# Placing the experts' rows tile by tile inside the output stage

## The chip, the cores and the metric

The kernel runs on one core of one Trainium2 chip, in one launch. The metric is the device time of that launch in microseconds (us). The core has five engines that run side by side, each taking its own instructions in order: TensorE (PE, matmuls; PEld is its loading of weights), VectorE (DVE), ScalarE (ACT), GpSimd (POOL) and SyncE (SP), which here only issues DMAs. ACT and POOL issue some DMAs too. The engines meet through semaphores.

## The reference, cut to what matters

Two layers run over 1024 latent tokens and 256 context tokens. In each, attention is merged and projected, and then every token goes through a mixture of experts: the best of 4 groups, the two best of its 8 experts, 32 experts in all. The last layer needs the 1024 latent tokens only.

```
x = x + mod[:, 2] * merge_branches(ya, yb, yc, gates, P)
h2 = modulate(rms_norm(x), mod[:, 3], mod[:, 4])
g_idx = argmax(h @ w_rg); e_in_group = (h @ w_re)[its group]
top_v, top_i = lax.top_k(e_in_group, 2)
w = softmax(top_v) * g_w
order = argsort(flat_e); xs = h[order // 2]
y = (silu(xs @ w_gate[e]) * (xs @ w_up[e])) @ w_down[e]
x = x + mod[:, 5] * segment_sum(y * w, tok)
```

## The kernel before

Tokens are worked on in tiles of 128 rows: nq = 10 tiles in layer 0, nq = 8 in layer 1. Each layer has a stage of projections, one of attention, one that merges the branches, and the experts' stage, `stage_experts`. That last one has four blocks, and all engines meet at the end of a block:

1. `output_and_route` (L1630). For each tile t PE does 48 matmuls of the output projection (L1806; L1793 for the first tile). DVE multiplies by the gate (L1752) and adds the residual (L1755), ACT squares (L1727) and takes the root (L1730), DVE scales and shifts (L1766, L1769): that is h, the experts' input. POOL stores it (L1707). PE transposes h (L1816), ACT copies the transpose (L1718), PE multiplies it by the router (L1824), and DVE copies the 36 logits away (L1743). PE's order is: output(t), router products of tile t-2, transposes of tile t-1. The first pair of tiles is written out, the next ones run in a hardware loop of two tiles a turn; layer 0's last two tiles (context) are written out again.
2. `deal_rows` (L1851). When the logits of all tiles are there, DVE chooses the experts of all tokens in wide instructions of up to 320 elements, PE counts with small matmuls how many rows stand before each (L1996), and DVE works out each row's place. A job is 128 rows of one expert. Job e < 32 holds the first 128 rows of expert e; the jobs behind hold what goes beyond 128. POOL then writes each token's number to its place in the DRAM table `token_of`, with one indirect DMA per tile and choice (L2010), 20 in layer 0 and 16 in layer 1. The first expert's weights are loaded meanwhile.
3. `run_experts` (L2024). Job by job: POOL loads 128 token numbers (L2105) and gathers their rows of h (L2110), PE transposes them (L2224) and multiplies (L2232 for gate and up, L2246 for down). The weights are split into a high part (ACT, L2137) and a low part (DVE, L2185; a quarter of all, the second half of down, by POOL, L2122), so that three passes give the precision wanted. SP loads the next weights (L2085) as soon as the split has freed their buffer. The jobs come in pairs, the number of pairs is read from memory by each engine at the start (`load_count`). There are 74 jobs in both layers together.
4. `combine` (L2277): gathers both results of each token and adds them up.

Far ahead of this, POOL clears the result table `ye` in the attention stage of layer 0 (L761): 52 DMAs of 512 KB. The same DMA engines carry the loads of that stage, which SP issues: keys (L774), queries (L777), values (L782). The scores' matmuls are L852.

## Time and profile before

| | us |
|---|---|
| median of 3 runs (5578.72 to 5581.25) | 5580.46 |
| the profiled execution | 5575.79 |
| its span | 5574.2 |
| PE busy, share of span | 4813.2 (86%) |
| DVE busy | 3091.8 (55%) |
| ACT busy | 2596.6 (47%) |
| POOL busy | 1159.4 (21%) |

The profiled execution is one run, whose span is what the trace covers. A row of the timeline gives the start, the length, the engine, the line of the kernel, what is written from what, and in brackets how long the engine stood idle before it and which event ended that.

### The profile page before, as it was taken

Reading aid. Unit: us, or ns where it says so; the run is one execution under the profiler, and the core shown is the slowest. Engines: PE = TensorE matmul, PEld = TensorE weight load, DVE = VectorE, ACT = ScalarE, POOL = GpSimd, SP = SyncE. Lnnn points to the kernel's source line nnn. Section 1 sums busy time; section 2 is a strip of 40 time slices with the busy share of each in tenths; the row PEclk is TensorE's granted clock in tenths of the full one; section 3 lists DMA queues with packets and bytes.
Section 4 is the critical chain, followed back from the end, with each engine's and each line's share of the span. In section 5 each row is a group of like instructions: output and inputs, shape, how many; then the busy total and the mean of one; then the engine's idle time right before and its main releaser. Section 6 shows DMA issues by size and latency. Waiting matters only on the chain. (4 is left out here: it accounts for less than half of the span.)

```text
span 5574.2 us, 82058 instructions
## 1 busy us (share of the span) xinstructions
PE 4813.2 (86%) x28941; PEld 4151.0 (74%) x28941; DVE 3091.8 (55%) x4784; ACT 2596.6 (47%) x3436; POOL 1159.4 (21%) x1097
## 2 busy tenths in 40 slices
PE   5788889889799986899992888999989998599994
PEld 0688878779687875787772888998878777487773
DVE  1655145666544443777766551557663433677775
ACT  0444245556423321777762442555652322477773
POOL 0444200340000001333333441004200000333332
PEclk7899999999899997999996999999989998799997
DMA  8533462313433364899986533424153325799997
GB/s 371 193 94 97 165 213 59 80 47 100 155 124 145 143 217 144 332 397 397 397 330 239 171 95 92 109 57 109 50 159 132 134 90 205 259 397 397 397 397 285
DMA packets 597494, 1111.13 MB, mean 199 GB/s; under 512 B 112560, under 2 KB 295632, under 8 KB 589104
## 3 DMA queue, kind: packets, MB, share of 16 engines
q1 hardware_dynamic: 551760, 956.16, 49.4%
q0 software_dynamic: 29504, 94.50, 4.3%
q10 hardware_dynamic: 16032, 57.88, 2.6%
q8 instruction: 119, 1.95, 0.1%
q14 instruction: 79, 0.65, 0.0%
HBM read 907.97 MB, written 200.45 MB: 199 GB/s over the span
## 5 line engine op out<-in xcount | busy, mean ns | idle before, releaser
L658 PE MATMUL project_proj_acc<-project_w_split,project_hT 128*128 128x256 f32 x5472 | 726.8, 293 | 0.0
L658 PEld LDWEIGHTS project_proj_acc<-project_w_split,project_hT 128*128 128x128 f32 x5472 | 696.2, 199 | 0.3 <-issue 0.2
L1538 PE MATMUL merge_acc<-merge_hT,merge_w_split 128*128 128x512 f32 (+1 forms) x2880 | 641.3, 377 | 36.4 <-DMA merge_hT<-hT 30.4
L1538 PEld LDWEIGHTS merge_acc<-merge_hT,merge_w_split 128*128 128x128 f32 x2880 | 506.6, 191 | 146.7 <-issue 29.7
L2185 DVE TENSOR_TENSOR experts_w_gate<-experts_raw_gate,experts_w_gate 128x2048 fp32r<-128x2048 f32 x148 | 373.5, 2531 | 356.1 <-ACT experts_w_gate L2137 355.9
L937 DVE TENSOR_REDUCE attend_stat<-attend_scores 128x1 f32<-128x1280 f32 (+2 forms) x288 | 305.9, 1062 | 325.2 <-PE attend_scores L852 324.2
L2122 POOL TENSOR_TENSOR experts_w_down<-experts_raw_down,experts_w_down 128x2048 fp32r<-128x2048 f32 x74 | 361.4, 4884 | 534.3 <-ACT experts_w_down L2137 534.3
L837 PE MATMUL attend_out_acc<-attend_values,attend_probsT 128*128 128x64 f32 x3904 | 468.3, 271 | 0.1
L837 PEld LDWEIGHTS attend_out_acc<-attend_values,attend_probsT 128*128 128x128 f32 x3904 | 459.3, 192 | 0.4 <-ACT attend_probsT L882 0.4
L2232 PE MATMUL experts_gate_acc<-experts_w_gate,experts_rowsT 128*128 128x512 f32 x1776 | 438.2, 402 | 12.3 <-DVE experts_rowsT L2190 6.0
L2246 PE MATMUL experts_result_acc<-experts_w_down,experts_hiddenT 128*128 128x512 f32 x1776 | 436.8, 401 | 12.2 <-DVE experts_w_down L2185 12.2
L2232 PE MATMUL experts_up_acc<-experts_w_up,experts_rowsT 128*128 128x512 f32 x1776 | 426.3, 395 | 0.0
L882 ACT COPY attend_probsT<-attend_scores 128x1024 f32<-128x1024 f32 (+1 forms) x288 | 216.5, 752 | 409.3 <-PE attend_scores L826 409.3
L2232 PEld LDWEIGHTS experts_gate_acc<-experts_w_gate,experts_rowsT 128*128 128x128 f32 x1776 | 331.1, 190 | 101.7 <-issue 19.1
L2137 ACT CAST experts_w_gate<-experts_raw_gate 128x2048 fp32r<-128x2048 f32 x148 | 282.3, 1912 | 264.2 <-DMA experts_raw_gate<-in_w_exp_gate_dram 193.0
L2246 PEld LDWEIGHTS experts_result_acc<-experts_w_down,experts_hiddenT 128*128 128x128 f32 x1776 | 330.6, 189 | 88.5 <-issue 12.6
L2232 PEld LDWEIGHTS experts_up_acc<-experts_w_up,experts_rowsT 128*128 128x128 f32 x1776 | 333.2, 188 | 81.2
L852 PE MATMUL attend_scores<-attend_keys,attend_queries 128*128 128x256 f32 (+2 forms) x1344 | 327.1, 358 | 63.9 <-DMA attend_queries<-qk 49.8
L1707 POOL DMA_DIRECT2D h<-experts_h_tile x18 | 9.8, 542 | 1663.0 <-DVE experts_h_tile L1769 1663.0
L2185 DVE TENSOR_TENSOR experts_w_up<-experts_raw_up,experts_w_up 128x2048 fp32r<-128x2048 f32 x148 | 331.8, 2283 | 1.2 <-ACT experts_w_up L2137 1.2
L1547 PE MATMUL merge_acc<-merge_yT,merge_w_split 128*128 128x512 f32 (+1 forms) x1440 | 319.3, 371 | 0.0
L1230 POOL TENSOR_TENSOR attend_p<-attend_p,attend_b_stat 128x640 f32<-128x640 f32 (+1 forms) x72 | 121.9, 1693 | 936.7 <-DVE attend_b_stat L1183 936.7
...
## 6 DMA issues: line engine op xcount, KB each, us to landing
experts_raw_gate<-in_w_exp_gate_dram SPq DMA_DIRECT2D x148, 1024.0 KB, 13.9
...
attend_keys<-qk SPq DMA_DIRECT2D x128, 320.0 KB, 5.7
...
```

Of the source, the lines that this page charges most:

```text
L658: m = pe.matmul(acc[s % 4][:, 0:HALF], hT[:, a, k, t * P:(t + 1) * P], w_split[hf][:, c, k, :], start=(i == 0 and k == 0), stop=(i == 2 an ...
L837: m = pe.matmul(acc[b][:, 0:HD], probsT[b][:, j, :], values[hb][:, kt, :], start=(j == 0), stop=(j == sx.n - 1))
L852: m = pe.matmul(scores[b][:, col:col + n * P], queries[hb][:, sx.t * P:(sx.t + 1) * P], keys[hb][:, half, a * P:(a + n) * P], start=(half ...
L882: act.copy(probsT[b][:, 0:n, :], scores[b][:, 0:n * P].rearrange("p (j n) -> p j n", n=P)).then_inc(ca.sem, 1)
L937: dve.tensor_reduce(stat[:, k, 0:1], scores[b][:, sx.cols], AX.X, ALU.max).then_inc(mx.sem, 1)
L1538: m = pe.matmul(acc[:, b, 0:w], w_split[b][:, a, k, :], hT[:, x, k, 0:w], start=(i == 0 and k == 0), stop=(i == 2 and k == KD - 1))
L1547: m = pe.matmul(acc[:, 3 + b, 0:w], w_split[b][:, a, KD + k, :], yT[:, x, b * KB + k, 0:w], start=(i == 0 and k == 0), stop=(i == 2 and k ...
L2122: pool.tensor_tensor(w[DOWN][:, 1, 1, :], raw[DOWN][:, 1, :], w[DOWN][:, 0, 1, :].bitcast(F32), ALU.subtract).then_inc(w_lo_pool.sem, 1)
L2137: act.copy(w[n][:, 0, half, :], raw[n][:, half, :]).then_inc(w_hi[n].sem, 1)
L2185: dve.tensor_tensor(w[n][:, 1, half, :], raw[n][:, half, :], w[n][:, 0, half, :].bitcast(F32), ALU.subtract).then_inc(w_lo[n].sem, 1)
L2232: m = pe.matmul(acc[:, :], xT[:, a, half * (KD // 2) + k, :], w[n][:, c, half, k * EH:(k + 1) * EH], start=(half == 0 and i == 0 and k == ...
L2246: m = pe.matmul(acc_y[:, c0 * 512:(c0 + 1) * 512], hT[:, a, half * (HK // 2) + k, :], w[DOWN][:, c, half, k * D + c0 * 512:k * D + (c0 + 1 ...
```

## The change

The clearing loop runs over the jobs 32 to 51 in place of 0 to 51: 20 DMAs instead of 52.

What was the block `deal_rows` is spread over its neighbours. In the output stage DVE now chooses the experts of tile t-1 (`choose`, 20 steps and a copy) and places tile t-2 (`place`, 7 steps), each step waiting for the one before it; PE does two small matmuls per tile that count (`ranks`); POOL writes the first 128 rows of each expert to the table, two indirect DMAs per tile (`scatter`). A row beyond 128 is sent to a spare part of the table instead. PE's transposes of tile t-1 now stand in the middle of output(t), and its router products right behind it. SP loads the router's constants ahead of the loop, and the first gate and up weights at its end; the first down weights follow in the next block.

In `run_experts` DVE counts the jobs first (`count_jobs`), then splits, and works out the places of the rows beyond 128 (`deal_beyond`) after the first splits; POOL writes them (`scatter_beyond`), two indirect DMAs after each of the pairs 1 to nq. The weights of the results are worked out at the end (`weights`).

```diff
         if clear_results:
             pool.memset(zeros[:, :], 0.0).then_inc(zeroed.sem, 1)
             pool.wait_ge(zeroed.sem, zeroed.done(0))
-            with pool.Fori(0, MAX_JOBS) as j:
+            with pool.Fori(NE, MAX_JOBS) as j:
                 pool.dma_start(scr["ye"][ds(j * P, P), :], zeros[:, :]).then_inc(cleared.sem, 16)
-            pool.wait_ge(cleared.sem, cleared.done(MAX_JOBS - 1))
+            pool.wait_ge(cleared.sem, cleared.done(MAX_JOBS - NE - 1))
...
-                deal_rows(nc, io, scr, l, nq, st, inner, logits, row_of, weight, jobs, more_pairs, raw, raw_in)
+                output_and_route(nc, io, scr, l, nq, st, inner, ident, r, scat, raw, raw_in)
...
+            sp.dma_start(r.small[:, :], io["k_small"]).then_inc(route_in.sem, 16)
+            sp.dma_start(r.token[:, :], io["k_token"]).then_inc(route_in.sem, 16)
+            sp.dma_start(r.aside[:, :, :], io["k_aside"]).then_inc(route_in.sem, 16)
+            sp.dma_start(earlier[:, :], io["k_earlier"]).then_inc(route_in.sem, 16)
             with sp.Fori(1, NL // 2) as p:
                 body(p, 0)
             if nq > NL:
                 body(NL // 2, 1)
+            for n in range(2):
+                for half in range(2):
+                    sp.dma_start(raw[n][:, half, :], expert_half(io, l, slice(0, 1), n, half)
+                                 ).then_inc(raw_in[n][half].sem, 16)
...
+            def scatter(t):
+
+                pool.wait_ge(rb.sem, rb.done(t * NB + NB - 1))
+                for c in range(2):
+                    pool.indirect_dma_start(
+                        out=scr["token_of"], out_offset=bass.IndirectOffsetOnAxis(
+                            ap=row_first[:, t, c:c + 1].bitcast(U32), axis=0),
+                        in_=r.token[:, t:t + 1], in_offset=None).then_inc(scat.sem, 16)
...
+                    if later(t, 2):
+                        scatter(t - 2)
...
+            pool.wait_ge(route_in.sem, route_in.done(3))
+            for p in range(nq // 2):
+                body(p, 0)
+            scatter(nq - 2)
+            scatter(nq - 1)
...
+            def choose(t, b):
+                n = [0]
+                def step(ins):
+                    ins.then_inc(ra.sem, 1)
+                    dve.wait_ge(ra.sem, ra.done(t * NA + n[0]))
+                    n[0] += 1
+                lgt, s, hot = logit[b], scratch[b], r.hot
+                g = lgt[:, 0:NG]
                 dve.wait_ge(lm.sem, lm.done(t))
-                dve.tensor_copy(logits[:, ds(t, 1), :].rearrange("p o n -> p (o n)"), lg[b][:, 0:N_ROUTE]
-                                ).then_inc(lc.sem, 1)
+                dve.tensor_copy(lgt[:, :], lg[b][:, 0:N_ROUTE]).then_inc(lc.sem, 1)
+                dve.wait_ge(lc.sem, lc.done(t))
+                step(dve.tensor_reduce(best[b][:, 0:1], g, AX.X, ALU.max))
+                step(dve.scalar_tensor_tensor(out=group[b][:, :], in0=g, scalar=best[b][:, 0:1],
+                                              in1=r.small[:, C_PICK4:C_PICK4 + NG], op0=ALU.is_equal, op1=ALU.mult))
+                step(dve.tensor_reduce(pick[b][:, 0:1], group[b][:, :], AX.X, ALU.max))
+                step(dve.tensor_scalar(group[b][:, :], group[b][:, :], pick[b][:, 0:1], 1.0, ALU.is_equal, ALU.subtract))
...
+                for c in range(2):
+                    chosen = hot[:, ds(t, 1), c, :].rearrange("p o n -> p (o n)")
+                    step(dve.tensor_reduce(best[b][:, 1 + c:2 + c], masked[b][:, :], AX.X, ALU.max))
+                    step(dve.scalar_tensor_tensor(out=s[:, :], in0=masked[b][:, :], scalar=best[b][:, 1 + c:2 + c],
+                                                  in1=r.small[:, C_PICK32:C_PICK32 + NE], op0=ALU.is_equal, op1=ALU.mult))
+                    step(dve.tensor_reduce(pick[b][:, 1 + c:2 + c], s[:, :], AX.X, ALU.max))
+                    step(dve.tensor_scalar(chosen, s[:, :], pick[b][:, 1 + c:2 + c], None, ALU.is_equal))
+                    if c == 0:
+                        step(dve.scalar_tensor_tensor(out=masked[b][:, :], in0=chosen, scalar=-3e30,
+                                                      in1=masked[b][:, :], op0=ALU.mult, op1=ALU.add))
+                hots = [hot[:, ds(t, 1), c, :].rearrange("p o n -> p (o n)") for c in range(2)]
+                if later(t, 2):
+                    dve.wait_ge(rk.sem, rk.done(t - 2))
+                step(dve.tensor_tensor(both[b][:, :], hots[0], hots[1], ALU.add))
+                if later(t, 1):
+                    dve.wait_ge(rk.sem, rk.done(t - 1))
+                step(dve.tensor_tensor(seen[b][:, :], seen[1 - b][:, :], both[b][:, :], ALU.add))
...
+                assert n[0] == NA, n[0]
+            def place(t, b):
+                n = [0]
+                def step(ins):
+                    ins.then_inc(rb.sem, 1)
+                    dve.wait_ge(rb.sem, rb.done(t * NB + n[0]))
+                    n[0] += 1
+                rank = r.rank[:, ds(t, 1), :].rearrange("p o c -> p (o c)")
+                row = r.row[:, ds(t, 1), :].rearrange("p o c -> p (o c)")
+                dve.wait_ge(rk.sem, rk.done(t))
+                step(dve.tensor_tensor(two[b][:, :, :], lg[b][:, RANK].unsqueeze(1).to_broadcast([P, 2, NE]),
+                                       r.hot[:, ds(t, 1), :, :].rearrange("p o c n -> p (o c) n"), ALU.mult))
+                step(dve.tensor_reduce(rank, two[b][:, :, :], AX.X, ALU.add))
+                step(dve.tensor_tensor(row, rank, first[b][:, :, 0], ALU.add))
...
+                step(dve.tensor_copy(row_first[:, ds(t, 1), :].rearrange("p o c -> p (o c)"), first[b][:, :, 3]))
+                assert n[0] == NB, n[0]
...
-                        take(t - 2, b)
+                        place(t - 2, b)
+                    if later(t, 1):
+                        choose(t - 1, 1 - b)
...
+            choose(nq - 1, 1)
+            place(nq - 2, 0)
+            place(nq - 1, 1)
+            dve.tensor_copy(r.total[:, :], lg[1][:, TOTAL]).then_inc(tot.sem, 1)
...
+                    if hf == 0:
+                        transposes(t - 1, 1 - b)
...
+            def ranks(t, b):
+                pe.wait_ge(ra.sem, ra.done(t * NA + NA - 5))
+                pe.matmul(lg[b][:, RANK], r.earlier[:, :], both[b][:, :], start=True, stop=False)
+                m = pe.matmul(lg[b][:, RANK], r.ones[:, :], seen[1 - b][:, :], start=False, stop=True)
+                if isinstance(t, int) and t == nq - 1:
+                    m = pe.matmul(lg[b][:, TOTAL], r.ones[:, :], seen[b][:, :], start=True, stop=True)
+                m.then_inc(rk.sem, 1)
...
                     if isinstance(t, int) and t == 0:
                         first_output()
+                        pe.wait_ge(const_in.sem, const_in.done(1))
                     else:
                         output(p, b)
-                    if isinstance(t, int) and t == 1:
-                        pe.wait_ge(const_in.sem, const_in.done(1))
+                        products(t - 1, 1 - b)
                     if later(t, 2):
-                        products(t - 2, b)
-                    if later(t, 1):
-                        transposes(t - 1, 1 - b)
+                        ranks(t - 2, b)
             body(0, 0)
             body(1, 0)
             with pe.Fori(2, NL // 2) as p:
...
+            for half in range(2):
+                sp.dma_start(raw[DOWN][:, half, :], expert_half(io, l, slice(0, 1), DOWN, half)
+                             ).then_inc(raw_in[DOWN][half].sem, 16)
...
+            def scatter_beyond(t):
+                for c in range(2):
+                    pool.indirect_dma_start(
+                        out=scr["token_of"], out_offset=bass.IndirectOffsetOnAxis(
+                            ap=row_beyond[:, t, c:c + 1].bitcast(U32), axis=0),
+                        in_=r.token[:, t:t + 1], in_offset=None).then_inc(scat2.sem, 16)
...
+            pool.wait_ge(scat.sem, scat.done(2 * nq - 1))
             gather(0, 0, 0)
             gather(1, 1, 0)
-            pairs(pool, n_pairs, body)
+            n_pairs = load_count(pool)
+            body(0, False)
+            pool.wait_ge(dealt.sem, dealt.done(0))
+            for i in range(1, nq + 1):
+                body(i, False)
+                scatter_beyond(i - 1)
+            body(nq + 1, False)
+            pool.wait_ge(scat2.sem, scat2.done(2 * nq - 1))
+            with pool.Fori(nq + 2, n_pairs - 1) as i:
+                body(i, False)
+            body(n_pairs - 1, True)
...
+            def count_jobs():
+                step(dve.memset(one_row[:, :], 1.0))
+                step(dve.tensor_tensor(more[:, :, :], r.total[:, :].unsqueeze(2).to_broadcast([P, NE, NT - 1]),
+                                       r.small[:, C_TILE + 1:C_TILE + NT].unsqueeze(1).to_broadcast([P, NE, NT - 1]),
+                                       ALU.is_gt))
...
+                dve.tensor_copy(more_pairs[:, :], pairs_f[:, 0:1]).then_inc(counted.sem, 1)
+            def deal_beyond():
+                step(dve.tensor_tensor(beyond[:, :], tiles_sum[:, :], tiles[:, :], ALU.subtract))
+                step(dve.tensor_tensor(beyond[:, :], beyond[:, :], r.small[:, C_JOB:C_JOB + NE], ALU.subtract))
+                step(dve.tensor_scalar(beyond[:, :], beyond[:, :], float(NE - 1), float(P), ALU.add, ALU.mult))
+                step(dve.tensor_tensor(r.hot[:, :, :, :].rearrange("p t c n -> p (t c) n"),
+                                       r.hot[:, :, :, :].rearrange("p t c n -> p (t c) n"),
+                                       beyond[:, :].unsqueeze(1).to_broadcast([P, 2 * nq, NE]), ALU.mult))
...
+                dve.tensor_copy(row_beyond[:, :, :].rearrange("p t c -> p (t c)"), f[3]).then_inc(dealt.sem, 1)
...
+            count_jobs()
             split(GATE, 0)
+            rows_lo(0)
             split(UP, 0)
-            rows_lo(0)
+            deal_beyond()
+            n_pairs = load_count(dve)
             pairs(dve, n_pairs, body)
+            weights()
```

PE, layer 0, tiles 1 and 2 of the output stage, before. out_acc is the output projection, hT_acc the transposes, logit_acc the router's products:

```order
L1806 MATMUL experts_out_acc<-experts_w_out,experts_mT 128x512 x48
L1816 MATMUL experts_hT_acc<-experts_ident,experts_h_tile 128x128 x8
L1806 MATMUL experts_out_acc<-experts_w_out,experts_mT 128x512 x48
L1824 MATMUL experts_logit_acc<-experts_w_router,experts_hT_tile 128x36 x8
L1816 MATMUL experts_hT_acc<-experts_ident,experts_h_tile 128x128 x8
```

The same tiles after the change:

```order
L1938 MATMUL experts_out_acc<-experts_w_out,experts_mT 128x512 x24
L1950 MATMUL experts_hT_acc<-experts_ident,experts_h_tile 128x128 x8
L1938 MATMUL experts_out_acc<-experts_w_out,experts_mT 128x512 x24
L1958 MATMUL experts_logit_acc<-experts_w_router,experts_hT_tile 128x36 x8
L1938 MATMUL experts_out_acc<-experts_w_out,experts_mT 128x512 x24
L1950 MATMUL experts_hT_acc<-experts_ident,experts_h_tile 128x128 x8
```

The transposes of tile 0 moved from behind the 48 matmuls of tile 1 to between their halves, and likewise for each tile after.

DVE in the loop of the output stage, after the change, from the end of one tile's h to the start of `choose`. The names behind "waits" are those under which a semaphore was first used, and mean nothing here; what matters is which rows wait:

```order
L1891 TENSOR_TENSOR experts_h_tile<-experts_h_tile,experts_shift_rows 128x1024 [waits project0_hT_hi]
L1855 ISA [waits project0_heads_stored1]
L1855 TENSOR_TENSOR experts_two<-experts_logit_acc,experts_hot 128x64
L1849 ISA
L1857 ISA [waits modulation_c_loaded]
L1857 TENSOR_REDUCE experts_rank<-experts_two 128x2
L1849 REGISTER_ALU
L1858 REGISTER_ALU [waits modulation_c_loaded]
L1858 TENSOR_TENSOR experts_row<-experts_rank,experts_first 128x2
L1849 REGISTER_ALU
L1859 SCALAR_TENSOR_TENSOR experts_first<-experts_rank,experts_row 128x2 [waits modulation_c_loaded]
```

Before, one copy (L1743) stood here. Now 27 steps and the copy do, with a register instruction between each two, since the number that a step waits for depends on the loop's turn; at some steps the register instruction itself waits, as at L1858.

POOL in the experts' jobs, after the change, pair 1 and the start of pair 2:

```order
L2117 TENSOR_TENSOR experts_w_down<-experts_raw_down,experts_w_down 128x2048
L2100 DMA experts_index<-token_of 128x1
L2105 DMA experts_rows<-h,experts_index 128x1024
L2117 TENSOR_TENSOR experts_w_down<-experts_raw_down,experts_w_down 128x2048
L2092 DMA token_of<-experts_token,experts_row_beyond 9216x1 x2
L2100 DMA experts_index<-token_of 128x1
L2105 DMA experts_rows<-h,experts_index 128x1024
```

The two scatters (L2092) stand between a subtraction and the next load of token numbers; before, nothing stood there.

## Rows read from the trace of the kernel before

**Rows 1.** Windows: busy us per engine, granted clock, DMA share, GB/s

```profile
2072.00:2166.00 94.00, 94.00 (x484) 78.90 (x482) 35.50 (x48) 15.87 (x28) 3.73 (x7) 1.00 0.54 177
...
2204.00:2232.00 28.00, 0.00 (x0) 0.00 (x0) 0.71 (x4) 0.00 (x0) 18.24 (x19) 0.50 0.02 0
...
2283.00:2320.00 37.00, 36.83 (x174) 29.83 (x173) 34.10 (x18) 28.52 (x21) 17.39 (x7) 1.00 1.04 395
```

**Rows 2.** Timeline, layer 0, from the last h to the first job

```profile
2172.77 1.22 DVE L1769 TENSOR_TENSOR experts_h_tile<-experts_h_tile,experts_shift_rows 128x1024 f32<-128x1024 f32 x1
...
2180.79 0.20 DVE L1743 COPY experts_logits<-experts_logit_acc 128x36 f32<-128x36 f32 x1 [6.58 <-PE experts_logit_acc L1824]
...
2202.91 1.03 POOL L2010 DMA_INDIRECT token_of<-experts_token,experts_row_of  x1 [20.61 <-DVE experts_ended L1973]
...
2227.02 0.96 POOL L2010 DMA_INDIRECT token_of<-experts_token,experts_row_of  x1 [0.31 <-issue]
...
2247.88 8.38 PE L2232 MATMUL experts_gate_acc<-experts_w_gate,experts_rowsT 128*128 128x512 f32 x24 [2.36 <-DVE experts_rowsT L2190]
...
2256.11 5.76 PE L2232 MATMUL experts_up_acc<-experts_w_up,experts_rowsT 128*128 128x512 f32 x24
```

**Rows 3.** Timeline, layer 1, the same places

```profile
4729.52 1.23 DVE L1769 TENSOR_TENSOR experts_h_tile<-experts_h_tile,experts_shift_rows 128x1024 f32<-128x1024 f32 x1
...
4777.48 0.96 POOL L2010 DMA_INDIRECT token_of<-experts_token,experts_row_of  x1 [0.30 <-issue]
...
4798.43 8.02 PE L2232 MATMUL experts_gate_acc<-experts_w_gate,experts_rowsT 128*128 128x512 f32 x24 [2.36 <-DVE experts_rowsT L2190]
```

**Rows 4.** Timeline, layer 0, output stage in its loop

```profile
2074.80 0.16 DVE L1760 RECIPROCAL experts_norm_stat<-experts_norm_stat 128x1 f32<-128x1 f32 x1 [0.27 <-ACT experts_norm_stat L1730]
2075.17 1.28 DVE L1766 SCALAR_TENSOR_TENSOR experts_h_tile<-experts_x_tile,experts_norm_stat,experts_scale_rows 128x1024 f32<-128x1024 f32 x1 [0.20 <-DVE experts_norm_stat L1760]
...
2083.39 1.23 DVE L1752 TENSOR_TENSOR experts_x_tile<-experts_out_acc,experts_gate_in_rows 128x1024 f32<-128x1024 f32 x1 [5.58 <-PE experts_out_acc L1806]
...
2086.07 1.01 ACT L1718 COPY experts_hT_tile<-experts_hT_acc 128x1024 f32<-128x1024 f32 x1 [11.30 <-PE experts_hT_acc L1816]
...
2088.17 0.15 DVE L1757 TENSOR_SCALAR experts_norm_stat<-experts_norm_stat 128x1 f32<-128x1 f32 x1 [2.29 <-ACT experts_square L1727]
...
2091.25 0.19 DVE L1743 COPY experts_logits<-experts_logit_acc 128x36 f32 x1
...
2097.26 1.23 DVE L1752 TENSOR_TENSOR experts_x_tile<-experts_out_acc,experts_gate_in_rows 128x1024 f32<-128x1024 f32 x1 [5.82 <-PE experts_out_acc L1806]
```

**Rows 5.** Timeline, a small DVE step of the block that deals the rows

```profile
2185.49 0.20 DVE L1914 TENSOR_TENSOR experts_g_exp<-experts_g_exp,experts_small 128x40 f32<-128x40 f32 x1
```

**Rows 6.** One line of DVE: ns min/median/max, first and last start

```profile
L1183 DVE TENSOR_SCALAR attend_b_stat<-attend_b_stat,attend_lambda x72: 256/273/278, 1014.7 to 3974.4; 128x1 f32<-128x1 f32 x72
```

**Rows 7.** Timeline, layer 0, tile 1 of the output stage

```profile
2044.33 11.75 PE L1806 MATMUL experts_out_acc<-experts_w_out,experts_mT 128*128 128x512 f32 x48
...
2055.95 1.23 DVE L1769 TENSOR_TENSOR experts_h_tile<-experts_h_tile,experts_shift_rows 128x1024 f32<-128x1024 f32 x1
...
2057.32 1.06 PE L1816 MATMUL experts_hT_acc<-experts_ident,experts_h_tile 128*128 128x128 f32 x8 [1.24 <-DVE experts_h_tile L1769]
```

**Rows 8.** One line, the clearing DMAs; columns as in rows 6

```profile
L761 POOL DMA_DIRECT2D ye<-attend_zeros x52: 531/531/740, 649.9 to 692.1; - x52
```

**Rows 9.** Timeline, attention of layer 0: SP's loads and PE behind them

```profile
733.56 20.38 SPq L774 DMA_DIRECT2D attend_keys<-qk  x4
...
761.63 2.49 PE L852 MATMUL attend_scores<-attend_keys,attend_queries 128*128 128x512 f32 x6 [16.35 <-DMA attend_queries<-qk]
...
765.09 1.49 PE L852 MATMUL attend_scores<-attend_keys,attend_queries 128*128 128x512 f32 x6
```

**Rows 10.** Timeline, experts' jobs of layer 0, POOL and DVE

```profile
2283.43 4.48 DVE L2185 TENSOR_TENSOR experts_w_up<-experts_raw_up,experts_w_up 128x2048 fp32r<-128x2048 f32 x2
...
2283.76 2.82 POOL L2110 DMA_INDIRECT experts_rows<-h,experts_index  x1 [5.79 <-DMA experts_index<-token_of]
...
2325.80 4.94 POOL L2122 TENSOR_TENSOR experts_w_down<-experts_raw_down,experts_w_down 128x2048 fp32r<-128x2048 f32 x1 [6.15 <-ACT experts_w_down L2137]
```

285 lines of the change are left out of this document (118 added, 167 removed).

## The prediction

> **What bounds the kernel now.** I read four views, in this order.
>
> The windows show three kinds of stretch [rows 1]. In the output stage PE is busy without a gap (94.00 of 94 us) and DVE is busy 35.50 us of them: PE bounds it. In the 28 us before the first job PE does nothing and POOL alone works. In the jobs themselves the DMA share is full, 395 GB/s, and PE nearly so: they run at the rate of the DMA, and a faster engine gains nothing there.
>
> The timeline of the handover gives the piece that the change attacks [rows 2, 3]. In layer 0 the last h ends at 2172.77 + 1.22 = 2173.99, and the first gate product starts at 2247.88: 73.9 us in which each step waits for the one before. Of them 6.8 go by until the last logits, 22.1 until the first scatter, 24.1 for the other 19 scatters (last start 2227.02, 1.27 us apart), and 20.9 from the last start to the first product. In layer 1 the same way is 4730.75 to 4798.43, 67.7 us.
>
> The timeline of one tile [rows 4] gives DVE's room: tile to tile 97.26 - 83.39 = 13.87 us, of which DVE stands 5.82 waiting for PE, so its own chain takes 8.05 us. The waits for ScalarE within that chain are not room: DVE takes its instructions in order.
>
> The waits of PE, largest first, lead to the attention of layer 0 [rows 8, 9]: 16.35 us for queries whose key loads SP took 20.38 us to hand over. 52 clears of 0.524 MB were issued from 649.9 to 692.1; that is 27.3 MB, 69 us at 395 GB/s [rows 1], and SP's loads queue among them.
>
> **The change, part by part.** All times are the profiled execution's, 5575.8 us; the median of the runs is 4.7 us (0.08%) above it, and I add the difference at the end.
>
> *Clearing.* 32 clears fewer are 16.8 MB, 42 us of DMA time ahead of the moment when PE wants the queries. The wait of 16.35 goes whole. With it goes part of a slow restart: the first 6 matmuls behind it take 2.49 us, the next 6 take 1.49. Together -17.3. Bounds: 0 (the wait has another cause) and -20 (some more slow matmuls).
>
> *Start of the output stage, a cost.* PE started tile 1 at 2044.33 and ran it through, 11.75 us; the h of tile 0 was ready at 2055.95 + 1.23 = 2057.18, so the transposes, behind all 48 matmuls, waited 1.24 [rows 7]. Now they stand after 24. PE is there at 2050.2 and waits until 2057.8 (0.6 later, for two memsets and a cast that DVE does first). After 7.6 us of idling I take PE at the lower clock (1.2 GHz; the granted clock is 0.50 in the idle stretch of rows 1): the 8 transposes, 1.06 at full clock, take 2.0, and the next 24 matmuls 8.4 as in the first gate product, against 5.76 for the 24 behind it [rows 2]. Tile 1 ends at 2068.2 instead of 2056.1. Router products of tile 0 (1.7) and tile 2 (12.3) follow: 2082.2, where it was 2069.5 (2083.39 less one period of 13.87). **+12.7 us**, in each layer, since the stage is the same code. Bounds: 8 (clock stays high, part absorbed later) and 13.
>
> *DVE in the loop, a cost.* A step of 40 elements takes 0.20, one with 1 element 0.15 [rows 4, 5], and starts 0.04 after the one before. A scalar from memory adds 0.06 (0.273 with two of them against 0.15 [rows 6]). `choose` is the copy and 20 steps: 7 tiny, 12 of 32, 2 of 64 elements, 7 of them with such a scalar: 4.3, and 21 gaps of 0.04: 5.1. `place` is 2 steps of 64 and 5 tiny: 1.5. Less the old copy, 0.2: +6.4. In the loop nine of a tile's register instructions wait themselves. The one of the trace that does (between L1760 and L1766) leaves 0.20 idle instead of 0.04 [rows 4]; other such places leave less, and I take 0.13: +1.1. In return ScalarE's copy of the transposes (1.01, just ahead of the square [rows 4]) moves to a time when it is idle: -0.65. DVE's chain becomes 8.05 + 6.4 + 1.1 - 0.65 + 0.1 for the branch = 15.0 us against PE's 13.87. DVE bounds the loop: +1.15 a tile. That is 6 tiles in layer 0, **+7**, and 5 up to the last tile in layer 1, **+6**. Written-out tiles (8, 9 of layer 0) have no register instructions: 13.9, level with PE. Bounds per tile: 0 (PE still sets the pace) and +3.5 (all 27 register instructions show at 0.13).
>
> *Behind the last h.* Place(7) and choose(8) take 6.6, then the last logits are there (7.0 after h, as before), choose(9) ends at 12.1, place(8) and place(9) at 15.1. POOL starts its last four scatters at 13.7, 15.0, 16.3, 17.5 after h. From the last start to the first product it took 20.9; the loading of the count now stands behind the gathers: 19.9. So the first product comes 37.4 after the last h instead of 73.9. In layer 1, with choose(6) and place(5) at the loop's price, 38.1 instead of 67.7. That is **-36.5** and **-29.6**. Counting the jobs and the first split on DVE, 4 + 4.5 us, lie in the 19.9; splitting up and `deal_beyond`, 4.5 + 4, lie behind the first gate product, 8.4, and what follows it.
>
> *In sum to the first product.* The last h moves by 12.7 + 7 - 0.65 = +19 in layer 0 and 12.7 + 6 - 0.65 = +18 in layer 1. Layer 0: -36.5 + 19 = -17.5. Layer 1: -29.6 + 18 = -11.6.
>
> *In the jobs.* `scatter_beyond` adds two scatters to 10 and 8 pairs, 2.5 us of POOL each at 1.27. POOL stood idle 6.15 before a subtraction that is PE's next need [rows 10]. The DMA moves no more than a few KB. I take +1.5 over both layers for gathers that come late; bounds 0 and 20. Setup of stages: nothing, the weights of the results are worked out while PE does the last down products.
>
> Sum: -17.3 - 17.5 - 11.6 + 1.5 = -44.9. 5575.8 - 44.9 = 5530.9, and by the median 5580.5 - 44.9 = 5535.6. I say **5536**.
>
> **Where a rule and the rows part.** The gap of 0.20 where a register instruction waits, against 0.04 [rows 4], is what makes DVE the bound. The Trainium skill, "VectorE: DVE Perf Modes", section "The DRAIN you can't avoid", says that a semaphore after each operation costs nothing extra. By that the chain would be 13.9, PE would keep the pace, and the sum would be rival 1's.
>
> A gather that POOL issued while DVE was in a 4.48 us pair of two-input subtractions took 2.82 us instead of about 1 [rows 10]. The Trainium skill, "SBUF — State Buffer", section "SBUF: two separate sides", says that GpSimd and such a DVE operation take turns at one port pair, for the whole instruction. By it each scatter in the jobs may be held until a subtraction ends: rival 4's way.
>
> **Rivals.**
>
> 1. *PE keeps the pace in the loop.* For it: 27 small steps and a register instruction that runs beside the step before would be hidden. Against: the 0.20. It gives 13 less: 5523.
> 2. *DVE is dearer than thought:* every register instruction shows. 18 more of 0.13 in 11 tiles are 26 us: 5562. Against: most stand ahead of a waiting step without waiting themselves.
> 3. *The wait for the queries stays*, since SP is late for another reason. Then 17 are lost: 5553. For it: SP's queue holds many loads of its own there. Against: 27.3 MB of zeros in front of them.
> 4. *Slower than before: the scatters in the jobs.* If each is held 0.96 + 4.48 = 5.4 us, a pair costs 10.9, less the slack of 6.15, times 18 pairs: +85, 5620. It decides from the point where a pair of scatters takes over 6.15 + 45/18 = 8.6 us. Against: one gather shows 2.82, which gives 5.6 a pair, within the slack.
> 5. *The stall at tile 1 is small,* as the clock doesn't fall: 5531.
>
> **How the numbers follow.** Forecast (with 5 in it) 0.55, rival 1 0.15, rival 2 0.12, rival 3 0.12, rival 4 0.06. The forecast's own range is 5526 to 5547. To leave out no more than 2 in 10 the range goes from 5517, a little below rival 1, to 5562, rival 2. A change of 0.2%, 11 us, is about the least that a measurement of this kernel can tell. Only rival 4, or 2 and 3 together, end above 5569: faster 0.92, same 0.04, slower 0.04.
>
> **What would show it.** The attention of layer 0: no wait of PE for queries after the first. Tile 1 of each output stage: PE idle 7 to 8 us before the transposes, then 24 matmuls at half the clock. The loop: 15.0 us from one L1874 to the next, without idle time for PE's products before it. Last h to first gate product: 37 to 38 us. The jobs: about 395 GB/s, as before. It is wrong if the loop's tiles take over 17 us, if the wait for queries is still there, or if PE waits for POOL's low part in the first 24 jobs.

## The result, and the profile after

| | before | after |
|---|---|---|
| median (us) | 5579.6 (4 runs, 5578.7 to 5581.3) | 5680.4 (4 runs, 5678.6 to 5696.4) |
| span of the profiled execution | 5574.2 | 5679.0 |

The change made the kernel 1.9% slower: ratio 1.0187, 95% interval 1.0168 to 1.0205. The forecast was 5536, range 5517 to 5562. Where the 104.8 us between the two spans lie, read from the starts of the h tiles and of the first gate product of each job in both timelines:

| stretch | after minus before (us) |
|---|---|
| up to the first h of layer 0 | -14.6 |
| first to last h, layer 0 | +19.5 |
| last h to first product, layer 0 | -32.5 |
| the 36 jobs of layer 0 (643.2 to 728.5) | **+85.3** |
| last job of layer 0 to first h of layer 1 | +5.0 |
| first to last h, layer 1 | +16.9 |
| last h to first product, layer 1 | -24.3 |
| the 38 jobs of layer 1 (679.8 to 728.2) | **+48.5** |
| what follows | +1.0 |

Outside the jobs 29.0 us were gained. Inside them 133.8 were lost, in the step that the prediction had put at 1.5.

The windows of the kernel after, in the output stage's loop, the handover and the jobs (columns as in [rows 1]):

```profile
2087.00:2163.00 76.00, 70.19 (x370) 57.96 (x369) 54.00 (x171) 11.84 (x20) 12.54 (x15) 1.00 0.63 205
2184.00:2212.00 28.00, 2.00 (x13) 1.78 (x13) 16.34 (x56) 7.64 (x6) 6.83 (x7) 0.50 0.35 116
2400.00:2500.00 100.00, 82.92 (x369) 67.20 (x368) 70.36 (x37) 61.58 (x45) 36.97 (x19) 0.91 1.01 313
```

In the loop PE, busy without a gap before, now is idle 8% of the time. In the jobs the DMA share is still full (1.01), but what it moves fell to 313 GB/s, from 396 in the same 100 us of the kernel before. In this trace a full share says that packets are under way, and not how many bytes come.

The handover of layer 0, and the ends of it in layer 1, in the timeline after (to [rows 2, 3]):

```profile
2177.70 1.22 DVE L1891 TENSOR_TENSOR experts_h_tile<-experts_h_tile,experts_shift_rows 128x1024 f32<-128x1024 f32 x1
...
2196.32 0.96 POOL L1738 DMA_INDIRECT token_of<-experts_token,experts_row_first  x1 [0.30 <-issue]
2200.59 0.58 POOL L2100 DMA_DIRECT2D experts_index<-token_of  x1 [3.32 <-POOLq L1691]
2207.69 1.83 POOL L2105 DMA_INDIRECT experts_rows<-h,experts_index  x1 [6.51 <-DMA experts_index<-token_of]
...
2220.29 8.27 PE L2291 MATMUL experts_gate_acc<-experts_w_gate,experts_rowsT 128*128 128x512 f32 x24 [2.36 <-DVE experts_rowsT L2247]
...
4809.13 1.23 DVE L1891 TENSOR_TENSOR experts_h_tile<-experts_h_tile,experts_shift_rows 128x1024 f32<-128x1024 f32 x1
...
4853.73 2.50 PE L2291 MATMUL experts_gate_acc<-experts_w_gate,experts_rowsT 128*128 128x512 f32 x5 [2.36 <-DVE experts_rowsT L2247]
```

From the end of the last h to the last scatter's start it is 17.4 us, from there to the first product 24.0; 41.4 together, and 43.4 in layer 1.

The jobs are where the time went. The time of a job is taken here from the start of its first gate product to that of the next job's. Before, a job took 18.1 us in the first ten and 18.5 from there on, but for the first two of a layer. After, the jobs whose rows are gathered behind a pair of scatters take 22 to 30 us (ten in layer 0: 28.2, 29.8, 27.9, 29.0, 28.7, 27.6, 26.4, 26.2, 28.1, 24.2; eight in layer 1: 30.1, falling to between 22.3 and 22.9 in the last three), all others 18.1. One such job in the timeline after (to [rows 10]):

```profile
2303.15 2.85 POOL L2092 DMA_INDIRECT token_of<-experts_token,experts_row_beyond  x1 [0.17 <-issue]
...
2306.31 1.87 POOL L2092 DMA_INDIRECT token_of<-experts_token,experts_row_beyond  x1 [0.30 <-issue]
2308.19 0.58 POOL L2100 DMA_DIRECT2D experts_index<-token_of  x1
...
2320.47 0.98 POOL L2105 DMA_INDIRECT experts_rows<-h,experts_index  x1 [11.71 <-DMA experts_index<-token_of]
...
2328.81 1.54 PE L2283 MATMUL experts_rowsT_acc<-experts_ident,experts_rows 128*128 128x128 f32 x6 [7.10 <-DMA experts_rows<-h,experts_index]
```

The two scatters hold POOL for about 5 us. Then the index load, 512 bytes, keeps POOL waiting 11.71 us instead of the 5.79 of [rows 10], the gather goes out late, and PE waits 7.10 for its rows. The DMA view of the same stretch of 200 us, after (GB/s in 40 slices of 5 us, then issues with their median time to landing):

```profile
GB/s 414 416 139 205 349 408 415 411 411 302 310 154 148 188 381 415 415 397 353 265 336 77 249 262 410 414 402 406 326 353 108 225 213 377 417 412 369 378 296 224
...
token_of<-experts_token,experts_row_beyond POOLq DMA_INDIRECT x10, 12.5
experts_index<-token_of POOLq DMA_DIRECT2D x9, 0.5 KB, 11.4
```

Behind each pair of scatters the whole stream of weights breaks down: it stays below 360 GB/s for 15 to 30 us, and its lowest slices of 5 us behind the first four pairs are at 139, 148, 77 and 108 GB/s. In the packet records of this stretch 173 of 17,792 packets of 2 KB took over 1 us (the longest 6.1; the median is 0.084), and 33 of 6,656 packets of 4 KB.

### The profile page after: what moved, and what is told of

Its sections match the earlier page's. It is cut to its first block and busy times, and to the rows that moved or that the text cites. A ratio compares the mean times of both kernels' runs of the same rounds, so it can differ in the third digit from the quotient of the medians.

```text
span 5679.0 us, 82433 instructions
## 1 busy us (share of the span) xinstructions
PE 4842.9 (85%) x28870; PEld 4177.9 (74%) x28870; DVE 3324.0 (59%) x5228; ACT 2593.5 (46%) x3436; POOL 1232.5 (22%) x1101
## 5 line engine op out<-in xcount | busy, mean ns | idle before, releaser
L2242 DVE TENSOR_TENSOR experts_w_gate<-experts_raw_gate,experts_w_gate 128x2048 fp32r<-128x2048 f32 x148 | 513.7, 3503 | 189.9 <-ACT experts_w_gate L2141 189.9
L2305 PE MATMUL experts_result_acc<-experts_w_down,experts_hiddenT 128*128 128x512 f32 x1776 | 459.2, 417 | 12.2 <-DVE experts_w_down L2242 12.2
L2305 PEld LDWEIGHTS experts_result_acc<-experts_w_down,experts_hiddenT 128*128 128x128 f32 x1776 | 349.7, 201 | 92.6 <-issue 12.6
L852 PE MATMUL attend_scores<-attend_keys,attend_queries 128*128 128x256 f32 (+2 forms) x1344 | 324.3, 356 | 48.5 <-DMA attend_queries<-qk 34.4
L894 ACT ACTIVATE attend_probs<-attend_scores,attend_stat 128x1280 f32<-128x1280 f32 (+2 forms) x288 | 284.3, 987 | 53.0 <-DVE attend_stat L945 37.1
```

Source lines behind the costliest of these rows:

```text
L852: m = pe.matmul(scores[b][:, col:col + n * P], queries[hb][:, sx.t * P:(sx.t + 1) * P], keys[hb][:, half, a * P:(a + n) * P], start=(half ...
L894: act.activation(probs[b][:, 0:sx.n * P], scores[b][:, sx.cols], ACT.Exp, scale=SCORE_SCALE, bias=stat[:, s % 4, 1:2], accum_out=stat[:, s ...
L2242: dve.tensor_tensor(w[n][:, 1, half, :], raw[n][:, half, :], w[n][:, 0, half, :].bitcast(F32), ALU.subtract).then_inc(w_lo[n].sem, 1)
L2305: m = pe.matmul(acc_y[:, c0 * 512:(c0 + 1) * 512], hT[:, a, half * (HK // 2) + k, :], w[DOWN][:, c, half, k * D + c0 * 512:k * D + (c0 + 1 ...
```

## The experiments

The theory after this reading, **Q**: the index load stands behind the scatters' slow packets on one queue. Rivals: **P**, POOL's own time for the scatters (the prediction's rival 4); **C**, the scatters' packets slow the other DMAs. From e5 on, **A**, which narrows C: what is slow is 4-byte writes to neighbouring addresses; **W** is its rival, by which 128 writes of 4 bytes cost this wherever they go. Every ratio is to the kernel before.

**e1: no scatters in the jobs** (the tokens of the rows beyond 128 are not written at all, so their jobs work on a wrong row, but on as many)

```diff
                 body(i, False)
-                scatter_beyond(i - 1)
```

> The changed kernel with the twenty (first layer) and sixteen (second layer) scatters of the rows beyond 128 left out of the jobs; jobs past the thirty-second then gather row 0 throughout, the work of each job stays the same. What is left out is only where the late rows' tokens are written. The trace after the change puts +85.3 us (first layer) and +48.5 us (second) into the jobs. If the scatters cause that, in whatever way, it goes: 5680 - 134 = 5546 us. If the jobs became slower for another reason (the six SP loads, the placing moved in front, the results no longer cleared), it stays near 5680.

Measured: 5519.9 us, 0.9894 (0.9878 to 0.9911). All jobs take 18.1 us but the first two of a layer. The scatters cost 160 us, more than the 134 seen in the comparison (I had expected 5546 us), because without them the jobs are 21 us *faster* than before (e16 tells why).

**e2: the scatters behind the first gather of a pair**

```diff
                         gather(g + 2, b, i + 1)
+                    if b == 0 and isinstance(i, int) and 1 < i <= nq + 1:
+                        scatter_beyond(i - 2)
```

> The same scatters, the same number per pair, but issued just behind a pair's first gather and ahead of POOL's subtraction, so that the next index load is issued some 15 us later instead of right behind them. Theory Q (the index load, on the same queue, stands behind the scatters' slowly landing packets: 11.7 us of idle before the gather instead of 5.2): the stalls go, about 5546 us. Theory P (POOL's own time for a pair of scatters, 4.7 us, is what the gather or the subtraction is late by): the time of POOL is the same, and now falls ahead of the subtraction that the down product waits for; the stalls stay, 5640 to 5720 us. Theory C (the scatters' packets slow the weight loads in the DMA engines): stays about 5680 us.

Measured: 5688.4, 1.0200 (1.0183 to 1.0217). Theory Q alone is refuted: nothing comes back, though a subtraction of POOL now stands between the scatters and the next index load. The window of the same stretch as above:

```profile
2400.00:2500.00 100.00, 86.20 (x371) 68.52 (x370) 63.84 (x36) 62.35 (x45) 41.40 (x20) 0.91 1.02 321
```

321 GB/s: the stream breaks down wherever the scatters stand. The loss is now spread over both jobs of a pair (19 to 28 us).

**e3: the index loads ahead of the loop**

```diff
+            pool.dma_start(ahead[:, :], scr["token_of"][2 * P:(2 * nq + 6) * P, :]...).then_inc(ahead_in.sem, 16)
...
-                pool.dma_start(index[b][:, :], scr["token_of"][ds(g * P, P), :]).then_inc(i_in[b].sem, 16)
+                rows = ahead[:, g - 2:g - 1]
```

> The scatters stay where the change has them; the index loads of jobs 2 to 25 (2 to 21 in the second layer) are taken out of the loop and come in one load behind the second gather. Theory Q: no index load stands behind a scatter, the stalls go: 5546 us, less or more by the one load (24 x 128 elements of 4 bytes; if it is late for job 2, some 10 us once in each layer). Theory P: POOL's scatters delay the gathers as before, about 5680 us, less what the index loads themselves cost. If the gather itself, queued behind the scatters' packets, is what is late, only part of the 134 us comes back, by the share of the 6.5 us that the gather still waits: 5600 to 5680.

Measured: 5601.9, 1.0042 (1.0025 to 1.0059). Half comes back, 78 us. So the queue is a part of it, and 82 us are left with no index load behind a scatter.

**e4: the clearing alone, on the kernel before**

```diff
-            with pool.Fori(0, MAX_JOBS) as j:
+            with pool.Fori(NE, MAX_JOBS) as j:
```

> The kernel before with one part of the change: only the results of jobs past the thirty-second are cleared. My theory (the PE waits 16.35 us for queries behind the clears' write traffic, and the trace after shows h0 14.6 us earlier): 5579.6 - 15 = 5565 us (5562 to 5566). Rival (the wait is given back by a later one): 5579 us.

Measured: 5562.5, 0.9971 (0.9959 to 0.9982), -16.0. In its timeline one wait of PE for queries is left (18.5 us, the first one of the stage); the one of [rows 9] is gone.

**e5: rows set aside 512 bytes apart**

```diff
-            "k_aside": (ASIDE + np.arange(NT)[None, :, None] * P + i[:, None, None]
-                        + T * np.arange(2)[None, None, :]).astype(np.float32),
+            "k_aside": (ASIDE + P * (np.arange(NT)[None, :, None] * P + i[:, None, None]
+                                     + T * np.arange(2)[None, None, :])).astype(np.float32),
```

> The changed kernel with the rows set aside 512 bytes apart instead of 4 (a constant table and the size of the array change; number, place and size of the scatters stay). Theory A (127 or so of a scatter's 128 elements go to neighbouring 4-byte slots, and that is what stops the 2 KB packets of the weights for up to 6 us): most of the 160 us that leaving the scatters out gave back comes, 5520 to 5560 us. Theory W (128 writes of 4 bytes cost this wherever they go): within 20 us of 5680.

Measured: 5539.1, 0.9929 (0.9912 to 0.9946). 141 of the 160 us come back by a table of numbers, with every instruction and every DMA in its place (the array in DRAM grows with it; in e9 it grows an eighth as much, to nearly the same time). Theory A holds, and W is refuted. The DMA view of the same 200 us:

```profile
GB/s 418 406 412 416 406 410 411 420 404 391 412 361 410 410 414 413 412 408 409 409 414 412 414 392 400 410 383 413 411 422 404 383 416 377 414 406 418 410 401 413
...
token_of<-experts_token,experts_row_beyond POOLq DMA_INDIRECT x12, 6.8
experts_index<-token_of POOLq DMA_DIRECT2D x12, 0.5 KB, 4.7
```

The breakdowns are gone, the scatters land in 6.8 instead of 12.5 us and the index load behind them in 4.7 instead of 11.4. And POOL is held as before:

```profile
2300.42 2.85 POOL L2092 DMA_INDIRECT token_of<-experts_token,experts_row_beyond  x1 [0.17 <-issue]
2303.57 1.87 POOL L2092 DMA_INDIRECT token_of<-experts_token,experts_row_beyond  x1 [0.30 <-issue]
2305.45 0.58 POOL L2100 DMA_DIRECT2D experts_index<-token_of  x1
2310.98 0.99 POOL L2105 DMA_INDIRECT experts_rows<-h,experts_index  x1 [4.96 <-DMA experts_index<-token_of]
```

So rival P is excluded as the cause of the 141: the same 2.85 and 1.87 us, and all jobs of layer 0 take 18.1 us but the first two. The index load now lands in 4.7 us behind the scatters, as it does in e1 without any: so Q's half was a consequence of A.

The 19 us that are left against e1 lie in four jobs of layer 1, at 21.8 to 23.0 us. They are those behind the scatters of the tiles 4 to 7, and what is special about these tiles stands in the routing. By the reference, with its inputs, 74 of 2560 rows of layer 0 lie beyond the first 128 of their expert, but 401 of 2048 in layer 1. These late rows go to their real places, which are neighbours in every version, since they follow one another in a job's list. e5's packet records for the 20 us behind each pair of scatters in layer 1:

| tile | 0 | 1 | 2 | 3 | 4 | 5 | 6 | 7 |
|---|---|---|---|---|---|---|---|---|
| late rows in the pair of scatters, of 256 | 0 | 0 | 0 | 4 | 57 | 94 | 116 | 130 |
| packets of 2 or 4 KB over 0.6 us | 1 | 5 | 2 | 3 | 19 | 23 | 30 | 40 |
| the late job, us | 18.1 | 18.1 | 18.1 | 18.1 | 21.8 | 22.7 | 23.0 | 22.9 |

The same goes for layer 0: tile 9, with 60 late rows, has 16 such packets, tiles 0 to 8 at most 5. So what is left looks like theory A once more, in the rows that can't be spread. There the index load is slow again and POOL has no slack left; behind tile 4:

```profile
5000.51 1.38 POOL L2105 DMA_INDIRECT experts_rows<-h,experts_index  x1 [7.34 <-DMA experts_index<-token_of]
5001.91 4.65 POOL L2117 TENSOR_TENSOR experts_w_down<-experts_raw_down,experts_w_down 128x2048 fp32r<-128x2048 f32 x1
```

No run places the late rows differently, so this last step isn't proved.

**e6 to e8: what else the scatter could be.** Each replaces the two scatters of a pair and leaves the writing of the late rows' tokens out. e6, a plain store to 512 contiguous bytes:

```diff
-                    pool.indirect_dma_start(out=scr["token_of"], out_offset=..., in_=r.token[:, t:t + 1], ...)
+                    pool.dma_start(scr["token_of"][ASIDE + (t + NT * c) * P:ASIDE + (t + NT * c + 1) * P, :],
+                                   r.token[:, t:t + 1]).then_inc(scat2.sem, 16)
```

> Each scatter in the jobs replaced by a plain store of the same 128 elements of 4 bytes into 512 contiguous bytes of the rows set aside, on the same queue; the late rows' tokens are not written. If small writes to neighbouring slots do it (A, or W), the time stays near 5680 us. If it is the indirect form (its descriptors made by POOL, its DMA_INDIRECT of 1.9 to 2.9 us on POOL), most comes back: near 5525 us.

e7, an indirect gather of as many elements:

```diff
+                    pool.indirect_dma_start(
+                        out=taken_back[:, 2 * t + c:2 * t + c + 1], out_offset=None, in_=scr["token_of"],
+                        in_offset=bass.IndirectOffsetOnAxis(ap=r.row_of[:, t, c:c + 1].bitcast(U32), axis=0)
```

> Each scatter in the jobs replaced by an indirect gather of 128 elements of 4 bytes from the placed rows into SBUF: same instruction on POOL, same queue, same number of elements, read instead of written; the late rows' tokens are not written. If the writing does it, near 5525 us. If the indirect form or the element count on the queue does it, near 5680 us.

e8, work of POOL without a DMA:

```diff
+                    pool.tensor_tensor(hold[:, :], hold[:, :], hold[:, :], ALU.subtract).then_inc(held.sem, 1)
```

> Each scatter in the jobs replaced by a POOL subtraction of 128x1024 on a tile of its own (about 2.4 us, so POOL is held some 4.8 us per pair as by the two scatters); no DMA of its own; the late rows' tokens are not written. Theory P of the prediction (POOL's time is what the pair has to fit into, and it fits): as without scatters, 5520 us, at most 5525. If POOL's occupation is what makes the gather late: 5600 us or more.

Measured: e6 5614.8 (1.0064, 1.0047 to 1.0080), e7 5525.2 (0.9905, 0.9888 to 0.9921), e8 5620.3 (1.0082, 1.0064 to 1.0100). Reading costs next to nothing (5 us over e1), writing neighbours without the indirect form 95: it is the writes, and the form isn't needed for it. (In e7's profiled execution, the slowest of its four at 5538.0 us, three jobs behind the tiles 5 to 7 of layer 1 were late by 4 us too; among the places read there are the neighbouring ones of the late rows.) That e6 is not as dear as the scatters (160) is not explained.

e8 went against what I expected. Its POOL rows:

```profile
2299.68 7.84 POOL L2095 TENSOR_TENSOR experts_hold<-experts_hold 128x1024 f32<-128x1024 f32 x2
2307.47 0.58 POOL L2100 DMA_DIRECT2D experts_index<-token_of  x1
2313.39 2.18 POOL L2105 DMA_INDIRECT experts_rows<-h,experts_index  x1 [5.34 <-ACT experts_w_down L2142]
```

A subtraction of 128x1024 took 3.9 us and not 2.4, so a pair held POOL 7.84 us. That is 3 more than the scatters' 4.7, and it costs 100 us. But e8 doesn't price POOL's time alone. DVE's two gate splits beside it took 8.59 us together instead of 6.88 in e5, so a part of the 100 is DVE's. That POOL's slack ends somewhere between 4.7 and 7.8 us a pair is likely and not shown.

**e9 and e13: how far apart** (64 and 16 bytes; the factor P of e5 becomes 16 and 4)

> As the run with the rows set aside 512 bytes apart, but 64 bytes apart: a scatter then writes into 8 KB instead of 64 KB or, in the change, 512 bytes. If only elements that share a line of some tens of bytes disturb each other: as with 512 bytes, 5539 us. If what counts is how narrow the range of addresses is: between 5539 and 5680.

> Rows set aside 16 bytes apart (4 bytes: 5680 us; 64 and 512 bytes: 5543 and 5539). If the elements disturb each other where they share a line of 64 bytes: four share one instead of sixteen, so clearly above 5543, some 5560 to 5640 us. If only directly adjacent words do (written together): about 5540.

Measured: 64 bytes 5542.5 (0.9936, 0.9921 to 0.9951), 16 bytes 5592.1 (1.0024, 1.0015 to 1.0034). With 4, 16, 64, 512 bytes between elements: 5680, 5592, 5543, 5539. Beyond 64 bytes there is next to nothing left to gain. That fits a cost by how many elements share 64 bytes, but the range into which a scatter writes grows along (512 bytes, 2, 8, 64 KB), and no run parts the two. 32 bytes was not tried.

**e14: the index load ahead of the scatters** (4 bytes apart as in the change)

```diff
                 body(i, False)
+                load_index(2 * i + 4, 0, i + 2)
                 scatter_beyond(i - 1)
```

> The changed kernel, rows aside 4 bytes apart as there, with the index load of the next pair issued ahead of the two scatters instead of behind them (ahead of POOL's own time for them, too). If the queue order is half of it, as the run with the index loads ahead of the loop showed (5602), about 5600 us. If the index load behind the scatters had nothing to do with it: 5680.

Measured: 5606.2, 1.0047 (1.0029 to 1.0065), as e3. Two ways of taking the load from behind the slow writes give 74 and 78 us.

**e10: tile 1's transposes behind its 48 matmuls** (on e5)

```diff
-                    if hf == 0:
+                    if hf == 0 and not (isinstance(t, int) and t == 1):
                         transposes(t - 1, 1 - b)
                 m.then_inc(mm.sem, 1)
+                if isinstance(t, int) and t == 1:
+                    transposes(0, 0)
```

> The kernel with the rows aside 512 bytes apart (5539 us) plus one edit in the output stage: for tile 1 alone the transposes of tile 0 stand behind all 48 matmuls, as before the change. My term: a stall of 7.6 us and 24 matmuls at the low clock (5 us more) go in each layer, 2 x 12.7, less what PE then waits for ACT's copy before the products (2 to 4 us): 5516 to 5522 us. Rival: from tile 2 on DVE sets the pace and had the stall as its own lead, so it is given back: 5535 to 5539.

Measured: 5531.2, 0.9916 (0.9903 to 0.9930), 8 below e5 and above the 5516 to 5522 that I expected; the two intervals overlap, and the timelines are clearer. First to last h takes 129.4 instead of 136.2 us in layer 0 and 100.5 instead of 107.7 in layer 1. Part is given back at once: h 1 comes 7.2 us behind h 0 instead of 16.4, but h 2 17.0 behind h 1 instead of 14.6. There DVE waits 4.38 us for PE, which in this order has stood 0.75 us for h and 1.10 us for ScalarE's copy of the transposes.

**e11: DVE's loop written out** (on e5)

```diff
-            pairs(dve, body)
+            for p in range(nq // 2):
+                body(p, 1 if p == NL // 2 else 0)
```

> The kernel with the rows aside 512 bytes apart (5539 us), with DVE's loop over pairs in the output stage written out, so that its waits are on constants and not on registers; the other engines keep their loops. My term: the register instruction ahead of each wait makes DVE's chain 15.0 us a tile, beside 13.9 to 14.6 of PE; written out, the six looped tiles of each layer fall to PE's pace: 5539 - 12 x (0.4 to 1.1) = 5526 to 5534 us. Rival: the loop's waits cost nothing or PE sets the pace already: 5539.

Measured: 5527.9, 0.9901 (0.9886 to 0.9916), 11 below e5, though the two intervals overlap a little. The timeline decides: from the third on all tiles take 14.1 to 14.3, where the looped ones took 14.6 to 15.9, and DVE, in its timeline, now waits for PE:

```profile
2091.53 1.23 DVE L1874 TENSOR_TENSOR experts_x_tile<-experts_out_acc,experts_gate_in_rows 128x1024 f32<-128x1024 f32 x1 [0.30 <-PE experts_out_acc L1939]
...
2105.80 1.23 DVE L1874 TENSOR_TENSOR experts_x_tile<-experts_out_acc,experts_gate_in_rows 128x1024 f32<-128x1024 f32 x1 [0.29 <-PE experts_out_acc L1939]
```

**e12 and e15: together.** e12 is e5 with e3's load ahead of the loop; e15 is e5 with the edits of e14, e10 and e11.

> Both edits that gave time back: rows aside 512 bytes apart (5539 us), and the index loads of the jobs 2 to 25 in one load ahead of the loop. If what is left of the scatters' cost (5539 against 5520 without them) is the gather that comes late in the second layer's jobs behind index load and scatters, it goes: 5518 to 5526 us. If it is the scatters' own packets: 5535 to 5540. The single load of 4-byte elements may cost up to 10 us of its own once per layer.

> All that gave time back together: rows aside 512 bytes apart, index load ahead of the scatters, tile 1's transposes behind its 48 matmuls, DVE's loop written out. From 5539: the late gathers of the second layer go (to 5520, the time without scatters), tile 1 gives 6 to 8 us and DVE's loop 11: 5500 to 5510 us. Rival: the jobs' gathers stay late by 4 us in a few jobs: 5515 to 5525.

Measured: e12 5530.8 (0.9915, 0.9901 to 0.9928), between its two forecasts: with no index load behind the scatters, six jobs of layer 1 around tiles 5 to 7 still take 18.6 to 19.7 us. e15 **5508.2 (0.9873, 0.9856 to 0.9891)**, as expected, 1.3% below the kernel before and 3.0% below the change.

**e16 and e17: why the jobs' own pace rose.** On e4. e16 shifts the stage's tiles to the addresses they have after the change, e17 the arrays in DRAM:

```diff
+        st.sb("shift", [P, 772 if nq == NT else 672])
```

```diff
+        ("token_of", (MAX_JOBS * P, 1), I32), ("apart", (2 * T, 1), I32),
```

> The kernel before with the clearing of the change (5562 us) and an unused tile ahead of the experts stage's tiles, so that the weights, rows and results of the jobs lie at the SBUF addresses that they have in the changed kernel. In every run with the new layout the jobs take 18.1 us, in the kernel before 18.5 from the tenth job on, with weight packets of 86 and 164 ns instead of 84 and 159. If the place in SBUF does it: jobs at 18.1, 20 us less, 5541 us. If not: 5562.

> The same (5562 us), with the arrays in DRAM that the change adds (an unused table among the inputs and 10 KB behind the list of tokens) instead of the tile in SBUF. If the place of the arrays in DRAM makes the packets shorter: 5541 us. If not: 5562. If neither this nor the shift in SBUF does it, the order of the loads or of the work does.

Measured: e16 5542.6 (0.9937, 0.9921 to 0.9954), e17 5561.3 (0.9974, 0.9963 to 0.9984). An unused tile is worth 20 us. The same window in e4 and in e16:

```profile
2400.00:2500.00 100.00, 99.64 (x461) 80.54 (x460) 72.28 (x42) 75.04 (x55) 36.98 (x17) 1.00 1.04 397
```

```profile
2400.00:2500.00 100.00, 100.00 (x466) 81.54 (x465) 86.62 (x44) 77.34 (x57) 37.13 (x17) 1.00 1.03 404
```

All jobs take 18.1 us but the first two of a layer. By the packet records the packets of 4 KB take 159 ns instead of 164, those of 2 KB 84 instead of 86. The weights land in 7.7 to 9.1 us instead of 12.0 to 14.0, and the wait of 2.2 us that ACT had for each job's gate weights is gone: the DMA no longer sets the pace.

The third number shows DVE busier, 86.6 of 100 us instead of 72.3. That isn't DVE becoming slower by the place of its tiles. ACT's part comes earlier, so the first gate split of each job now starts in the middle of POOL's subtraction. Rows of e4, then of e16:

```profile
2420.62 4.81 POOL L2122 TENSOR_TENSOR experts_w_down<-experts_raw_down,experts_w_down 128x2048 fp32r<-128x2048 f32 x1 [6.88 <-ACT experts_w_down L2137]
2425.09 2.49 DVE L2185 TENSOR_TENSOR experts_w_gate<-experts_raw_gate,experts_w_gate 128x2048 fp32r<-128x2048 f32 x1 [4.14 <-ACT experts_w_gate L2137]
...
2418.33 4.83 POOL L2123 TENSOR_TENSOR experts_w_down<-experts_raw_down,experts_w_down 128x2048 fp32r<-128x2048 f32 x1 [6.58 <-ACT experts_w_down L2138]
2420.70 4.61 DVE L2186 TENSOR_TENSOR experts_w_gate<-experts_raw_gate,experts_w_gate 128x2048 fp32r<-128x2048 f32 x1 [2.04 <-ACT experts_w_gate L2138]
```

The DVE row ends 2.15 us behind the end of POOL's in both: 2425.43 and 2427.58, 2423.16 and 2425.31. The second gate split, with no subtraction of POOL beside it, takes 2.3 us in both kernels.

## Why the prediction was wrong, step by step

- **In the jobs** ("The DMA moves no more than a few KB. I take +1.5 over both layers"): this step failed. It asked how long the scatters hold POOL, and how many bytes they move. On the first it said 2.5 us a pair; it was 4.7, and still within the slack in layer 0 (e5). On the second it was right, and that didn't help. It did not ask *where* the elements go. In layer 0 97% of the elements of these scatters go to the spare rows, 4 bytes apart, in layer 1 80%. Measured price: 141 us for the neighbourhood (change minus e5), of which 74 to 78 through the index load behind them (e3, e14), and 19 for the rest (e5 minus e1), all in the jobs of layer 1 behind tiles with many late rows.
- **Also left out**: the jobs' pace. The prediction took 395 GB/s for the chip's limit in this stage, "as before". It was the limit with the tiles at their old addresses. Worth -20 (e16), in the other direction.
- **Clearing** -17.3: -16.0 in e4. Right.
- **Start of the output stage** +12.7 a layer: the stall came as described, a little smaller (6.12 us of idling instead of 7.6, then 24 matmuls in 7.58 us instead of 8.4, with a granted clock of 0.50 up to 2048.1), rows below. By h 2 the stage is late by 10.6 us in layer 0 and 9.4 in layer 1 against the kernel before. The term was too high by 2 to 3, within its bounds. Undoing it gives only 6.8 and 7.2 by the last h (e10), since the old order has waits of its own when the products stand right behind it.

```profile
2042.63 1.97 PE L1950 MATMUL experts_hT_acc<-experts_ident,experts_h_tile 128*128 128x128 f32 x8 [6.12 <-DVE experts_h_tile L1891]
2044.26 7.58 PE L1938 MATMUL experts_out_acc<-experts_w_out,experts_mT 128*128 128x512 f32 x24
```

- **DVE in the loop** 15.0 us a tile: the looped tiles took 14.6 to 15.9, 15.1 in the mean. Right, and for the reason given: with constants in place of registers (e11) PE sets the pace at 14.2. DVE's rows of the loop after (to [rows 4]) show both: the wait for PE before L1874 is gone, DVE comes from its own last step, and the gap of 0.20 is there.

```profile
2081.28 1.22 DVE L1874 TENSOR_TENSOR experts_x_tile<-experts_out_acc,experts_gate_in_rows 128x1024 f32<-128x1024 f32 x1 [0.19 <-DVE experts_first L1840]
...
2096.92 1.23 DVE L1874 TENSOR_TENSOR experts_x_tile<-experts_out_acc,experts_gate_in_rows 128x1024 f32<-128x1024 f32 x1 [0.65 <-DVE experts_first L1840]
...
2102.06 1.29 DVE L1888 SCALAR_TENSOR_TENSOR experts_h_tile<-experts_x_tile,experts_norm_stat,experts_scale_rows 128x1024 f32<-128x1024 f32 x1 [0.20 <-DVE experts_norm_stat L1882]
```

  So rival 1 fell. The Trainium skill's rule behind it ("VectorE: DVE Perf Modes", section "The DRAIN you can't avoid") says that a semaphore after each operation costs nothing extra. It fits e11, where each wait's value is a constant and the small steps start 0.03 to 0.04 us behind the end of one another. It doesn't carry over to this loop, where the value comes from a register: there nine gaps of a tile are 0.12 to 0.19 us long, foretold nine of 0.13. In all, first to last h grew by 19.5 and 16.9, foretold 19 and 18. That is partly luck: the start was 2 to 3 us cheaper than foretold, and the tiles behind h 2 cost 8.9 us more than before in layer 0 and 7.5 in layer 1, foretold 6.4 and 5.4.
- **Behind the last h** 37.4 and 38.1: it was 41.4 and 43.4. The scatters' end came as worked out (last start 17.4 behind h, foretold 17.5). From there to the first product it was 24.0 us, foretold 19.9. The first index load kept POOL waiting 6.51 us, where it was 2.63 before; I had taken the whole way from the last scatter over from the rows of before, in which nothing else was under way (DMA share 0.02, now 0.35). That this is the reason isn't shown.
- **Rival 4** named the right place, the right sign and a size of +85, and got 6 in 100. Its mechanism wasn't what happened: it had each scatter held for 5.4 us, and they took 2.85 and 1.87. e8 shows that a neighbouring one exists: 7.8 us of POOL a pair, with DVE's splits longer beside them, cost 100 us. Where the trace of before showed 5.6 us against a slack of 6.15, two unknowns side by side, a chance several times as high would have been in order.

By these measurements the sum closes to 9 us: clearing -16, place in SBUF -20, output stages and handovers -13.0 and -7.4, spare rows +141, rest of the scatters +19, between the layers and behind +6: +110, against 101 by the medians. The difference is about what one stretch varies between executions: the first h started at 2035.9 to 2041.4 in kernels that are alike up to there. Of the 5.0 us between the layers 3.2 are there by the end of layer 1's merging stage, in stages that the change doesn't touch; they were not followed up.
